# Values projected with tokens on the partitions in a two-layer encoder: token tiles stationary, 384 or 256 weight columns moving, and no transposes of values

## The reference

```
h = rms_norm(x, norm_mix_pre[l]);  z = h @ w_in[l]
a_q, a_kv, a_kr, b_q, b_k, b_v, c_q, c_k, c_v = jnp.split(z, splits, axis=-1)
# group A, 4 heads: latent attention
kv = (rms_norm(ckv, kv_norm) @ w_ukv).reshape(b, s, 4, 64 + 64)
k  = concat([kv[..., :64], rotated kr]);  v = kv[..., 64:]
# group B, 4 heads: v = zv (256 columns of w_in), dilated windows, relative bias
# group C, 8 query heads over 2 key/value heads: v = zv (128 columns of w_in)
out = softmax(q k^T * scale) v
...
x = x + rms_norm(concat(A, B, C) @ w_out);  x = x + rms_norm(ConvGatedMLP(rms_norm(x)))
```

## Time and profile before

| what | value |
|---|---|
| median of 3 runs | 3733.16 us (3732.81 to 3735.91) |
| profiled execution | 3736.56 us |
| its span | 3734.7 us |
| PE busy | 3638.0 us, 97% |
| PEld busy | 3008.3 us, 81% |
| DVE, ACT, POOL busy | 1846.1, 1564.6, 1138.5 us |
| mean granted TensorE clock | 0.988 |
| head projections, first and second layer | 137.2 to 321.8, and 1980.7 to 2166.7 us |
| attention, first and second layer | 325.0 to 800.5, and 2169.7 to 2644.0 us |
| DMA | 233.99 MB, mean 63 GB/s |

### The profile page before, as it was taken

The page is one execution under the profiler, slowest core; times in us unless marked ns, Lnnn a source line. Parts: engine busy times, 40 slices in busy tenths (PEclk is TensorE's granted clock), DMA queues, the critical chain, the costliest instruction groups (busy, mean ns, idle before and its releaser), DMA issues. The chain is left out here.

```text
span 3734.7 us, 49829 instructions
## 1 busy us (share of the span) xinstructions
PE 3638.0 (97%) x18267; PEld 3008.3 (81%) x18267; DVE 1846.1 (49%) x2900; ACT 1564.6 (42%) x2527; POOL 1138.5 (30%) x827
## 2 busy tenths in 40 slices
PE   8999999989999999999999999999899999999998
PEld 7787777768788888888767877777788888888886
DVE  4135868954543333444551367699363333344335
ACT  4344878974311222221342367789552221221213
POOL 1233443433412221221342334433343221221213
PEclk9999999999999999999999999999999999999999
DMA  5442321023111111111324323110231111111113
GB/s 172 126 108 67 77 66 33 22 69 102 46 34 45 39 34 39 34 45 34 113 67 142 97 71 81 47 40 26 68 102 46 40 37 36 39 39 34 34 45 113
DMA packets 205964, 233.99 MB, mean 63 GB/s; under 512 B 15968, under 2 KB 164486, under 8 KB 205767
## 3 DMA queue, kind: packets, MB, share of 16 engines
q1 hardware_dynamic: 205807, 231.93, 21.1%
HBM read 173.86 MB, written 51.48 MB: 60 GB/s over the span
## 5 line engine op out<-in xcount | busy, mean ns | idle before, releaser
L222 PE MATMUL ps<-hh,wh 128*128 128x512 f32 (+1 forms) x2688 | 969.9, 361 | 15.4 <-PEq L216 11.5
L223 PE MATMUL ps<-hl,wh 128*128 128x512 f32 (+1 forms) x2688 | 955.9, 356 | 0.0
L224 PE MATMUL ps<-hh,wl 128*128 128x512 f32 (+1 forms) x2688 | 954.9, 355 | 0.0
L2466 POOL TENSOR_TENSOR wl<-raw,wh 128x1024 fp32r<-128x1024 f32 x126 | 301.7, 2401 | 1267.2 <-ACT wh L2299 1267.2
L222 PEld LDWEIGHTS ps<-hh,wh 128*128 128x128 f32 x2688 | 510.7, 190 | 93.8 <-issue 18.0
L2527 DVE SCALAR_TENSOR_TENSOR cb<-ps,params,cb 128x1023 f32<-128x1023 f32 (+1 forms) x172 | 143.9, 878 | 870.4 <-ACT cb L2308 870.4
L223 PEld LDWEIGHTS ps<-hl,wh 128*128 128x128 f32 x2688 | 511.0, 190 | 76.3 <-issue 5.7
L224 PEld LDWEIGHTS ps<-hh,wl 128*128 128x128 f32 x2688 | 510.1, 190 | 72.1
L1557 DVE TENSOR_TENSOR pl<-ps,ph 128x512 fp32r<-128x512 f32 (+1 forms) x576 | 375.0, 652 | 54.3 <-ACT ps L1402 53.9
L1511 DVE TENSOR_REDUCE mx<-ps 128x1 f32<-128x512 f32 x480 | 330.5, 689 | 141.8 <-PE ps L1316 82.9
L1401 ACT ACTIVATE ph<-ps 128x512 fp32r<-128x512 f32 (+1 forms) x576 | 329.6, 572 | 157.5 <-PE ps L1282 152.3
(11 more groups left out here) (265 smaller groups left out, 5644.8 us busy)
## 6 DMA issues: line engine op xcount, KB each, us to landing
raw<-in_w_up SPq DMA_DIRECT2D x88, 512.0 KB, 3.9
heads<-stage SPq DMA_DIRECT2D x38, 640.0 KB, 3.1
raw<-in_w_down SPq DMA_DIRECT2D x44, 512.0 KB, 3.7
rq<-heads SPq DMA_DIRECT2D x56, 320.0 KB, 4.8
raw<-in_w_in SPq DMA_DIRECT2D x32, 512.0 KB, 4.4
rk<-heads SPq DMA_DIRECT2D x32, 320.0 KB, 4.7
raw<-in_w_out SPq DMA_DIRECT2D x16, 512.0 KB, 4.3
residual<-my SPq DMA_DIRECT2D x32, 256.0 KB, 2.0
```

Of the source, the lines that this page charges most:

```text
L222: pe.matmul(out, wh, xh, start=(k == 0), stop=False)
L223: pe.matmul(out, wh, xl, start=False, stop=False)
L224: last = pe.matmul(out, wl, xh, start=False, stop=(k == len(pairs) - 1))
L2466: pool.tensor_tensor(c.wl[slot][:], c.raw[parity][:], c.wh[slot][:].bitcast(F32), ALU.subtract).then_inc(w_lo, units)
```

## The change

Values come out with tokens on the partitions. In both value products the token tile (128 tokens of `hh`/`hl`, or of `lath`/`latl`) is now the stationary operand, and the weight columns move: 256 in latent projections, 384 in head projections. The results are stored in a new tensor `values` (1280 rows of 640 columns), and a head's 64 columns are loaded from it as a tile of 128 partitions by 10 by 64. VectorE splits them from SBUF to `vh` and `vl`, with two instructions per head instead of four and no transpose.

In latent projections the last two units become five groups of two token tiles (30 matmuls of 256 columns), each copied by ScalarE (512 columns) and stored. In head projections the three value units become ten token tiles of 24 matmuls of 384 columns; all of the three weight chunks have to be split (`wv_hi`, `wv_lo`) before the first of them starts, where before each unit waited for its own chunk. GpSimd's splits of these chunks wait until the last rotation is done, since `wv_lo` lies where `rot` and `st2` were. The pieces of head 0 stand between the matmuls of the token tiles. In attention the values pieces leave the list of side work, and VectorE splits the next head's values at the end of step 9.

```diff
@@ product order, head projections, TensorE
+                pe.wait_ge(w_lo, LOADS - 2)
+                for t in range(NT):
+                    pe.wait_ge(evacuated, UNITS - 1 if t < 3 else UNITS if t < 6 else UNITS + t - 5)
+                    ts = slice(t * P, t * P + P)
+                    product(pe, bank(c, VALUE_BANKS[t % 6], V_COLS),
+                            [(c.hh[:, k, ts], c.hl[:, k, ts], c.wv_hi[:, k, :], c.wv_lo[k // 5][:, k % 5, :]) for k in range(KC)],
+                            lambda k: side(KC * t + k)).then_inc(w_used, 1)
@@ head projections, ScalarE
-                    if n == FIRST_SIDE - 1:
-                        for b in range(3):
-                            first_high(b)
+                    if n >= UNITS - 3:
+                        for u in ((0,), (1, 2), ())[n - UNITS + 3]:
+                            act.wait_ge(raw_arrived[(UNITS + u) % 2], 16 * ((UNITS + u) // 2))
+                            act.activation(c.wv_hi[:, :, u * P:u * P + P], c.raw[(UNITS + u) % 2][:], ACT.Copy).then_inc(w_hi, 1)
+                for b in range(3):
+                    first_high(b)
...
+                    act.activation(value_stage(t), bank(c, VALUE_BANKS[t % 6], V_COLS), ACT.Copy).then_inc(evacuated, 1)
@@ head projections, GpSimd
+                    if n >= UNITS - 3:
+                        for u in ((0,), (1, 2), ())[n - UNITS + 3]:
+                            cols = slice(u * P, u * P + P)
+                            raw = c.raw[(UNITS + u) % 2]
+                            pool.wait_ge(w_hi, UNITS + u - 1)
+                            pool.wait_ge(roped, len(ROPED))
+                            pool.tensor_tensor(c.wv_lo[0][:, :, cols], raw[:, 0:5, :], c.wv_hi[:, 0:5, cols].bitcast(F32), ALU.subtract)
+                            pool.tensor_tensor(c.wv_lo[1][:, :, cols], raw[:, 5:KC, :], c.wv_hi[:, 5:KC, cols].bitcast(F32),
+                                               ALU.subtract).then_inc(w_lo, 1)
@@ latent projections, TensorE (30 matmuls of 256 columns) and ScalarE
+                for g in range(5):
+                    pe.wait_ge(evacuated, 7 if g < 3 else 8)
+                    for i in range(2):
+                        ts = slice(256 * g + P * i, 256 * g + P * i + P)
+                        last = product(pe, bank(c, VALUE_BANKS[g], 256, off=256 * i),
+                                       [(c.lath[:, 2, ts], c.latl[:, 2, ts], c.kv_hi[:, 256:512], c.kv_lo[:, 256:512])])
+                    last.then_inc(unit_done, 1)
...
+                    act.activation(value_stage(g), bank(c, VALUE_BANKS[g]), ACT.Copy).then_inc(evacuated, 1)
@@ new helpers
+def value_columns(c, col):
+    return c.s_v[:, col:col + 64].rearrange("(t p) n -> p t n", p=P)
+def split_head_values(dve, c, slot, n):
+    dve.tensor_copy(c.vh[slot][:, :, 0:64], c.vt[:]).then_inc(c.v_hi, 1)
+    dve.wait_ge(c.v_hi, n + 1)
+    dve.tensor_tensor(c.vl[slot][:, :, 0:64], c.vt[:], c.vh[slot][:, :, 0:64].bitcast(F32), ALU.subtract).then_inc(c.v_lo, 1)
@@ attention
-        if i in (3, 11) and h >= 0 and new_kv(h + 1):
-            work.append(("values", h + 1, (i - 3) // 8))
...
-                    sp.wait_ge(v_turned, 2 * n)
-                    sp.dma_start(c.vt[0:64, :], c.s_z[vrow:vrow + 64, :]).then_inc(v_raw, 16)
+                    sp.wait_ge(v_lo, n)
+                    sp.dma_start(c.vt[:], value_columns(c, column)).then_inc(v_raw, 16)
...
+                def split_values(h):
+                    dve.wait_ge(v_raw, 16 * (kv_count(h) - 1))
+                    if h >= 2:
+                        dve.wait_ge(pv_done, NS * (h - 1))
+                    split_head_values(dve, c, kv(h), kv_count(h) - 1)
...
+                    if i == 9 and new_kv(h + 1):
+                        split_values(h + 1)
```

More of the change, by code:

```diff
@@ L179, in place_buffers @@
     assert at[0] <= end, (at[0], end)
+    at[0] = vl_end
+    c.wv_lo = [take("wv_lo0", [P, 5, V_COLS], F32R)]
+    assert at[0] <= projections_end
+    at[0] = vt_end
+    c.wv_hi = take("wv_hi", [P, KC, V_COLS], F32R)
+    c.wv_lo.append(take("wv_lo1", [P, KC - 5, V_COLS], F32R))
+    c.v_last = take("v_last", [P, V_COLS])
+    assert at[0] <= probabilities_end
     at[0] = arena
@@ L788, in _ @@
                 act.activation(c.lath[:, 2, :], c.lat[2][:], ACT.Copy).then_inc(lat_hi, 1)
-                for j in range(1, 8):
+                for j in range(1, 6):
                     m = 3 + j
@@ L909, in _ @@
                 sp.dma_start(c.rq[64:96, :], c.s_z[QAR + 32:QAR + 64, :]).then_inc(c.q_raw, 16)
-                for n in range(UNITS - 4, UNITS - 2):
-                    store(n)
+                store(UNITS - 1)
                 sp.wait_ge(c.k_lo, 3)
@@ L1104, in _ @@
                     first_maximum(j)
-                for part in range(2):
-                    first_values(part)
+                dve.wait_ge(head0, 16 * 5)
+                split_head_values(dve, c, 0, 0)
         end_phase(nc, raw_arrived + [w_hi, w_lo, w_used, tables, evacuated, squared, unit_sum, sum_read, turn_read,
@@ L1549, in _ @@
                             take_max(head, j, side_bank[what, head, j])
-                        elif what == "values":
-                            split_values(head, j, side_bank[what, head, j])
                     if 0 <= g < G_TOTAL:
```

145 lines of the change are left out of this document (68 added, 77 removed).

## The result

| | kernel before | changed kernel |
|---|---|---|
| median of 5 runs each (us) | 3732.81 (3730.74 to 3735.91) | 3712.97 (3709.93 to 3716.49) |
| ratio, with its 95% interval | | 0.9947 (0.9936 to 0.9958) |
| profiled execution / its span (us) | 3736.6 / 3734.7 | 3712.7 / 3710.1 |

The change is worth 19.8 us by the medians and 23.8 by the two profiled executions; the profiled one of before was the slower of its kind. The prediction was 3706, 27.6 less than before. A second measurement of the changed kernel (experiment 12) gave 3713.26.

The account below looks back on a forecast made before the run. TensorE, 97% busy, was taken to bound the kernel. Per layer 14.7 + 1.2 - 0.4 - 1.1 - 0.3 - 0.3 = 13.8, both layers 27.6, giving 3706 us; range 3699 to 3712, with rivals 1 and 2 3698 to 3720.

Parts of the forecast that it names:

- The transposes: Attention: removing them saves TensorE 0.85 plus 0.45 us per set, nine sets a layer, 11.6; head projections 1.3 more.
- Rival 4: Attention: transposes were hidden because VectorE bounds it, so removing them gives nothing; 3733 to 3731 us; chance 0.03.
- the half-clock stretch ends by the wall clock: First value set in attention: eight transposes take twice as long at clock 0.50, but removing them gives back about 0.7.
- The next maximum and low part are queued behind ... 2.4 us of slack: VectorE's split in attention: 1.5 us less 0.36 idle is hidden by 2.4 of slack; 0.3 charged per layer.
- low-part waits of over 5 us: Attention: TensorE's waits for VectorE's low parts above 5 us per layer would show the prediction's mechanism wrong.
- Small late steps ... 1.8 per layer: Attention: late steps behind the transposes, where VectorE splits values before going on, also go; 1.8 us per layer.
- Ends of stages: Smaller last ScalarE copies shorten TensorE's stops after head projections by 0.67 and latent projections by 0.57; 1.2 per layer.
- the smaller stores come no faster than TensorE makes their tiles: Value stores, five and ten of them: claimed paced by TensorE, with SyncE's last store issued after the last copy as before.
- The gate: Before the first token tile in head projections: TensorE waits for all three chunks' low parts, 1.1 us per layer.
- Rival 1: Value tiles in head projections: low parts late, stop 2.5 and clock falls, 4.2 instead of 1.4 per layer; 3711; chance 0.17.
- Rival 2: Attention: shared SBUF port with GpSimd stretches VectorE's split, 3.9 us in all, 5.7 lost per layer; 3717; chance 0.07.
- Rival 3: Attention: the `vt` load in 256-byte pieces lands after the 29.5 us available; 3769 at 33 us; chance 0.03.

Follow-up runs that it names:

- experiment 12: The changed kernel itself, unaltered, measured again beside the others on the same chip: 3713.26 us, ratio to kernel before 0.9951.
- experiment 9: Changed kernel with idle transposes of a constant tile put back at steps 3 and 11 of nine heads: 3733.92 us, ratio to kernel before 1.0004.
- experiment 1: Kernel before, with 16 of the 20 transposes of two heads' values left out in attention: 3729.69 us, ratio 0.9989.
- experiment 6: Changed kernel with the values' split of all heads but the first on GpSimd at step 14, not VectorE at step 9: 3708.43 us, ratio 0.9932.
- experiment 4: Changed kernel with VectorE splitting one token tile in place of ten for every set after the second: 3708.67 us.
- experiment 7: Changed kernel with ScalarE's second copy of the keys of heads 4 to 7 at steps 8 to 10 in place of 0 to 2: 3710.32 us.
- experiment 8: Changed kernel with VectorE taking second low-part pieces of value chunks 1 and 2, and ScalarE issuing the last latent-projection value store: 3710.68 us.

## Why the prediction was right or wrong

The range and the direction held; the time was 7 us too low. That it came so close is in part luck. In the two profiled executions the half-clock stretch at the start of attention was 6.8 us shorter in both layers, which gave some 4.0 of their 23.8. The sum had no term for it, and the prediction named it only as a reason to come out below 3706. What it gave in the executions behind the medians is not known. By part, in us per layer, layer 1 and layer 2:

| part | predicted | measured |
|---|---|---|
| attention | -13.4 less 0.3 for the split | -11.1, -10.0 |
| head projections (transposes, other cut, gate, slow clock behind it) | +0.4 | -0.3, -1.6 |
| stop before attention | -0.67 | -0.97, -0.75 |
| latent projections and the stop behind them | -0.5 | +1.84, +0.92 |

The rest of the 23.8 lies in stages that were not changed (1.9). Stretches at half clock fall differently from run to run: the 1.6 in head projections of layer 2 is one (6.8 us at half clock before, 3.4 after), and 1.07 of the 1.84 lies in latent projections of layer 1 ahead of the stop, where the half-clock stretch overlaps the part that is measured by 6.7 in place of 4.5; the like part of layer 2 differs by 0.07. The stop itself grew by 0.77 and 0.84. With the clock's 2.5 and 1.5 taken out, attention gained 8.6 and 8.5 where 13.1 was forecast, so the shortfall there is 4.5 per layer and not the 2 to 3 of the table.

**The transposes: right.** 0.85 and 0.45 from start distances is what group B lost, and what came back with idle ones. That this is TensorE's own time and not VectorE's is what experiment 9 shows. Rival 4 (hidden transposes, 3731 to 3733) is dead for the changed kernel. Of the kernel before as it stood, experiment 1 shows it to be true for seven of the eight transposes in groups A and C: there the split ahead of the low part was next in line by 0.05 us. The gain needed both halves of the change, and I had weighed the first alone. For the first set I had written that the half-clock stretch ends by the wall clock, so that removing eight transposes gives back 0.7; no row shows what ends it, and with them gone it was 6.8 shorter, and head 0 gained 3.10 and 2.07 where 1.15 had been put down for its transposes.

**"The next maximum and low part are queued behind ... 2.4 us of slack": wrong, and this is the step that failed.** I took the low part at 389.48 for that of the step begun one before 389.35. It is that of the step before that one: VectorE's order puts the maximum of step g + 1 ahead of the low part of step g, and the maximum at 388.87 belongs to the step begun at 387.72. So the low part is wanted at 391.0, not at 392.63. Worked out from the starts of all scores and low parts, in the heads of group A the low part is ready 0.83 ahead of the scores three steps on, 1.3 in group B and 0.6 in C. A split of 1.30 less 0.35 of idle time overdraws that; it shows at the low parts of steps 10 and 11 (0.05 ahead, against 0.85 and 0.20 without the split), because step 13 is short and step 11 no longer pauses. The split's own duration, 1.31, was even less than the 1.5 I took. Charged 0.3, it costs 2.9 (experiment 6; in heads 1 to 3 and 11 experiment 4 gives the same). The sign I had named for this, low-part waits of over 5 us, read 1.9: the loss is too finely spread to stand in the records as waits.

**"Small late steps ... 1.8 per layer": half right.** Steps 4 and 5 gained 0.2 to 0.5 in heads 1 to 3 and 11, 1.2 together. What I did not ask is who would be late next where 0.85 goes: in head 3 it is ScalarE with the table (1.22 given back, experiment 7), in head 11 the backlog at step 7 (0.4).

**Ends of stages: one right, one wrong in sign.** Before attention the copy of 384 columns set the end, as forecast. At the end of latent projections "the smaller stores come no faster than TensorE makes their tiles" was the failing sentence: TensorE makes what goes into one (six matmuls of 0.12) in 0.72, and SyncE needs 0.8 to issue it, so the stores queue up. ScalarE's last copy does end earlier behind the last matmul, by about 0.6, but SyncE ends 1.36 behind that copy. I had priced the copy and not the issue.

**The gate: right in kind, half in size.** 0.57 for 1.1. The chain has the links that I had written down: a rotation of 1.49 in place of 2.90, the last load landing in 4.4 where I took 5.0, GpSimd's two pieces in 2.6. The whole stage began 0.86 later (138.08 for 137.22). Counted from there, the low parts were ready 0.3 sooner than I had put it, by the load, and unit 8 ended 0.1 later. Rival 1 is dead.

**Rival 2 (port held)** named a real effect, and a part of the 2.9 is its doing. In heads 0 to 2 the loss at steps 12 to 14 is the split's length from start to end, less 0.97. In head 1 the split takes 1.34 and 0.36 is lost; in head 2, 1.46 and 0.49. In head 0 the splits of 1.42, 1.63, 1.68, 1.86, 1.92, 2.05, 2.71 and 2.73 (the changed kernel and experiments 7, 8 and 12) lose 0.46, 0.66, 0.72, 0.89, 0.97, 1.08, 1.75 and 1.77. So of the 0.9 in head 0, 0.5 comes from GpSimd beside it, and so does 0.1 in head 2, and up to 0.9 more in other runs. The rest is there without it, since the unstretched split in head 1 loses 0.36 and the one in head 11, at 1.42, loses 1.01. The reading on which this rival was built was also loose by 0.14: 1.49 and 1.55 make 3.04, and the multiplication took 2.90.

**Rival 3 (values late from device memory): dead.** The load of 1280 pieces landed in 3.8 us as the median and 8.1 at worst, and was needed some 28 after its issue.

## What to carry to other kernels

Before an engine's work is moved, write down for each result by how much it is ready ahead of the instruction that needs it, matched by index and not by nearness in time; an engine at 81% can have 0.8 us of room, or 0.05. Time taken off the bounding engine is worth only what the next one allows at that very step: test the removal and its inverse (the work put back idle), since the two answer different questions. When one large transfer becomes several small ones at the end of a stage, the issuing engine's time per transfer is a term of the sum.

## What the runs showed of the hardware that I had not expected

- A group of small transposes between 512-column products costs 0.41 for the first, with the products at its sides, and 0.063 for each further one (worked out in experiment 1).
- VectorE's cast of 640 f32 elements from SBUF took 0.48, while 512 from PSUM took 0.68; the subtraction of 640 took 0.83. The Trainium skill, "Advanced Engine Details and Errata", section "VectorE Performance Modes", has casts between SBUF tiles at two elements per cycle and subtractions not; the rows agree.
- SyncE took 0.77 to 0.82 to issue a store of 256 rows, ScalarE 0.40 for the same store (one row, experiment 8).
- Two engines on the shared port lengthened each other in both directions: VectorE's subtraction of 0.83 became 1.11 (head 0 of the changed kernel) or 1.79 (the same place in experiment 12), GpSimd's cast of 0.39 became 0.99.
